# Splitting the tie marking of the last row group's attention between POOL and DVE

## What is computed

```
rel   = relu(einsum(q_idx, k_idx))           # 8 indexer heads
score = einsum(w_idx, rel)                   # one score per query and key
score = where(causal, score, -inf)
_, idx = lax.top_k(score, 256)               # 256 keys per query, the earlier key on a tie
att   = q . k[idx] / 8 - slope[head] * (t - idx)
p     = softmax(att);  out = p . v[idx]      # 8 heads, one shared key/value head
```

## Time and profile before

| | us |
|---|---|
| runs of the kernel before | 3487.24, 3488.33, 3494.06; median 3488.33 |
| profiled execution, its own time | 3487.1 |
| span of the profile | 3485.3 |
| mean granted TensorE clock | 0.974 of full speed |
| PE busy | 3214.4 (92%) |
| DVE busy | 2173.1 (62%) |
| ACT busy | 1185.6 (34%) |
| POOL busy | 715.5 (21%) |

### The profile page before, as it was taken

One profiled execution on the slowest core, in us unless ns is written; L12 is line 12 of the kernel. 1 busy time (PEld: TensorE's weight loads), 2 busy tenths in 40 slices (PEclk: granted clock), 3 DMA queues, 4 the chain that ended last, 5 costly groups with the idle time before them and its releaser, 6 DMA issues.

```text
span 3485.3 us, 41580 instructions
## 1 busy us (share of the span) xinstructions
PE 3214.4 (92%) x15045; PEld 2625.6 (75%) x15045; DVE 2173.1 (62%) x3645; ACT 1185.6 (34%) x2030; POOL 715.5 (21%) x482
## 2 busy tenths in 40 slices
PE   6991799999999999999999889999999967889998
PEld 5871688778887888768887778875888856768886
DVE  2758827688824827599894872759999988710001
ACT  3331541253335631261112753127111156521111
POOL 3430110035767000001214200000211231001212
PEclk9995899999999999999999999999999989999999
DMA  6970475569996365545555126552555510255554
GB/s 218 303 252 0 177 258 197 189 230 290 290 290 233 134 227 204 183 148 193 193 193 181 67 86 228 208 183 93 194 193 194 197 49 20 108 196 194 194 194 165
DMA packets 177565, 640.14 MB, mean 184 GB/s; under 512 B 11293, under 2 KB 95305, under 8 KB 115560
## 3 DMA queue, kind: packets, MB, share of 16 engines
q1 hardware_dynamic: 160512, 574.66, 47.8%
q10 hardware_dynamic: 16872, 63.01, 4.7%
HBM read 476.14 MB, written 161.48 MB: 183 GB/s over the span
## 4 chain that ended last, share of the span: by engine, by line
PE 65%; DVE 15%; issue 12%; ACT 5%; DMA 2%; POOL 1%; DVEq 0%; ACTq 0%; SPq 0%; POOLq 0%
PE PS L1385 14%; PE PS L1356 13%; PE PS L1358 13%; PE PS L1357 13%; DVE flags L1145 2%; DVE probs L1245 2%; PE PS L1504 2%; PE PS L1370 1%; DVE W L1130 1%; PE PS L1371 1%; PE PS L1372 1%; ACT probs L806 1%; DVE PT L1253 1%; DVE W L1253 1%; PE PS L1339 1%
## 5 line engine op out<-in xcount | busy, mean ns | idle before, releaser
L1145 DVE TENSOR_SCALAR_CACHE_REDUCE flags<-W,cand 128x1408 uint8<-128x1408 f32 (+3 forms) x462 | 683.4, 1479 | 53.7 <-DVE cand L1172 40.0
L1385 PE MATMUL PS<-WS,HT 128*128 128x512 f32 x2088 | 483.4, 392 | 5.2 <-POOL WS L452 3.0
L1385 PEld LDWEIGHTS PS<-WS,HT 128*128 128x128 f32 x2088 | 394.3, 189 | 88.3 <-issue 3.8
L523 POOL TENSOR_TENSOR TMP<-TMP 128x512 f32<-128x512 f32 x88 | 114.7, 1304 | 1539.4 <-ACT TMP L875 1539.4
L1356 PE MATMUL PS<-HF,WS 128*128 128x512 f32 x1072 | 418.1, 390 | 4.4 <-DVE HF L939 2.5
L1358 PE MATMUL PS<-HF,WS 128*128 128x512 f32 x1072 | 417.8, 390 | 0.0
L1357 PE MATMUL PS<-HF,WS 128*128 128x512 f32 x1072 | 417.8, 390 | 0.0
L452 POOL TENSOR_TENSOR WS<-RAW,WS 128x1024 fp32r<-128x1024 f32 x116 | 279.6, 2410 | 612.7 <-ACT WS L595 581.5
L1356 PE MATMUL PS<-HT,WS 128*128 128x512 f32 x824 | 325.7, 395 | 0.8 <-POOL WS L452 0.8
L1358 PE MATMUL PS<-HT,WS 128*128 128x512 f32 x824 | 321.4, 390 | 0.0
L1357 PE MATMUL PS<-HT,WS 128*128 128x512 f32 x824 | 321.1, 390 | 0.0
(11 more groups left out here) (218 smaller groups left out, 6040.7 us busy)
## 6 DMA issues: line engine op xcount, KB each, us to landing
WS<-split_weights_scratch SPq DMA_DIRECT2D x234, 1024.0 KB, 4.8
split_weights_scratch<-WS SPq DMA_DIRECT2D x116, 1024.0 KB, 5.0
W<-split_weights_scratch SPq DMA_DIRECT2D x114, 1024.0 KB, 4.8
RAW<-in_w_in SPq DMA_DIRECT2D x34, 512.0 KB, 6.0
RAW<-in_w_ffn_gate SPq DMA_DIRECT2D x22, 512.0 KB, 6.3
RAW<-in_w_ffn_up SPq DMA_DIRECT2D x22, 512.0 KB, 6.3
RAW<-in_w_ffn_down SPq DMA_DIRECT2D x22, 512.0 KB, 5.7
W<-in_x ACTq DMA_DIRECT2D x4, 2048.0 KB, 11.7
```

What stands on the lines that cost most here:

```text
L523: nc.gpsimd.tensor_tensor(out=TMP[:, s, :], in0=TMP[:, s, :], in1=TMP[:, 2 + s, :], op=ALU.mult).then_inc(h_prod, 1)
L1145: step(nc.vector.tensor_scalar(flags[:, 0:n], SC[:, t, 0:n], cand[:, t:t + 1].bitcast(f32), 0.0, op, ALU.add, accum_out=count[:, t:t + 1]))
L1385: ins = mm(PS[:, 2 * t + half, :], lhs, split(c, w_part)[:, half * 512:(half + 1) * 512], start=first and part == 0 and w_part == 0, stop= ...
```

## The change

For the last group only, POOL makes the tie flags, the rank test, the product and the kept flags of each unit, and DVE is left with the scan and the carry. DVE's part comes after both heads of a turn. POOL's tie flags of a unit are issued after the unit before it is finished, and after `finish_rows` for the first unit of tile 2. Two semaphores are added. Groups 0 to 2 are as they were.

```diff
@@ gpsimd, stage C
                         for s, w in units(b):
                             t = b % RT
-                            pool.wait_ge(marked, MASK_BASE[g] + (t - 1) * (g + 1) + s // 512 + 1)
                             sc = SC[:, t, s:s + w]
+                            if g + 1 == GROUPS:
+                                u = (t - 1) * (g + 1) + s // 512 + 1
+                                tie, rank, kth = ties[:, 0, 0:w], ties[:, 1, 0:w], cand[:, t:t + 1].bitcast(f32)
+                                pool.wait_ge(m0_ready, (g + 1) * (g + 2) // 2)
+                                nc.gpsimd.tensor_scalar(tie, sc, kth, None, ALU.is_equal).then_inc(tie_ready, 1)
+                                pool.wait_ge(tie_ready, u)
+                                pool.wait_ge(ranked, u)
+                                chained(nc.gpsimd.tensor_scalar(rank, rank, room[:, t:t + 1], None, ALU.is_le))
+                                chained(nc.gpsimd.tensor_tensor(out=tie, in0=tie, in1=rank, op=ALU.mult))
+                                chained(nc.gpsimd.tensor_scalar(sc, sc, kth, None, ALU.is_le))
+                                chained(nc.gpsimd.tensor_tensor(out=sc, in0=sc, in1=tie, op=ALU.subtract))
+                            else:
+                                pool.wait_ge(marked, MASK_BASE[g] + (t - 1) * (g + 1) + s // 512 + 1)
                             chained(nc.gpsimd.tensor_scalar(sc, sc, -BIG, float(s - b * P), ALU.mult, ALU.add))
@@ vector
+            def rank_ties(t, b, u):
+                n = (t - 1) * (b // RT + 1) + u + 1
+                w = units(b)[u][1]
+                tie, rank = ties[:, 0, 0:w], ties[:, 1, 0:w]
+                dve.wait_ge(tie_ready, n)
+                ins = nc.vector.tensor_tensor_scan(rank, tie, tie, carry[:, 0:1] if u else 0.0, ALU.add, ALU.bypass)
+                if u + 1 < len(units(b)):
+                    chained(ins)
+                    ins = nc.vector.tensor_copy(carry[:, 0:1], rank[:, w - 1:w])
+                ins.then_inc(ranked, 1)
@@ vector, stage C, turn i
-                        marking = t < RT and u_mark < U and not marks_ahead(g)
+                        marking = t < RT and u_mark < U and g == 0
@@ vector, stage C, at the end of turn i
                         while marking and step < MARKS:
                             mark(t, RT * g + t, u_mark, step)
                             step += 1
+                        if g + 1 == GROUPS and t < RT:
+                            rank_ties(t, RT * g + t, u_mark)
```

More of the change, by code:

```diff
@@ L222, in build_block @@
         bit_step, topk_done, dist_ready = sem("bit_step"), sem("topk_done"), sem("dist_ready")
+        tie_ready, ranked = sem("ties_found"), sem("ties_ranked")
         mark_step, marked0, marked, m0_ready, m_ready, s_psum, s_masked, exp_done = sem("mark_step"), sem("first_keys_marked"), sem("keys_marked"), sem("first_mask_ready"), sem("mask_ready"), sem("s_psum"), sem("scores_masked"), sem("exp_done")
```

## The result

The changed kernel took 3495.34 us (median of 20 runs) against 3488.29 us for the kernel before (20 runs): ratio 1.0016, 95% interval 1.001 to 1.0023. It is slower by 7.05 us, just over what can be told from no change. The forecast was 3498 us with a range from 3486 to 3516. The profiled execution of the changed kernel took 3495.57 us, its span is 3493.8.

What follows compares the result with a forecast made beforehand. The prediction took DVE to bound the marked turns, then PE. Gain -20.3, border waits +17.4, finish_rows wait +12.3 and PE's clock +1.5 make +10.9 us: forecast 3498 us, range 3486 to 3516.

Steps and rivals of the forecast that it cites:

- both mechanisms: In the last group, DVE waits for POOL's masks at new row tiles (17.4 us) and behind `finish_rows` (12.3 us).
- marking of the kernel before: In the last group's turns, all marking was said to cost 23.1 us, 20.3 of it gained by the change.
- scan and carry, exposed: At the end of turns, 0.25 us of the 1.4 us left on DVE stays exposed, 2.8 us in 11 turns.
- waits at the borders: At each new row tile, DVE stands still for POOL's mask: 4.8, 6.3 and 7.8 us.
- wait behind `finish_rows`: At the end of turn 4, the scan waits 12.8 us for tie flags that POOL makes after `finish_rows`.
- work that runs ahead, and PE's clock: At the four waits, 0.5 us off each for copies and transposes; one low-clock stretch adds 1.5 us in turn 4.
- the cheap rival: POOL's comparisons cost only what immediate-scalar work does, so waits are shorter: +6.0 us, 3493 us; chance 0.23.
- the prediction's upper bound of 24.5: Bound on the gain in the last group's turns: all nominal time of what leaves DVE comes off, 24.5 us.
- The ring: Rival: POOL's and DVE's cycle per unit outlasts a turn, so inner turns wait: 3505 to 3533 us; chance 0.17.
- The faster rival: Inner turns fall to DVE's own work, 10.9 us for 14 tiles: -12.7 us, 3480 with cheap comparisons; chance 0.09.
- Absorbed waits: Rival: PE and ACT run ahead of a stalled DVE, four times 1.5 us more off: 3492 us; chance 0.06.
- Contention of POOL: In the last group's turns, POOL's work beside DVE's remaining instructions was said to add nothing.

Runs made afterwards that it cites:

- e5: The changed kernel without any marking of row tiles 1 to 3 of the last group, on both engines; ratio 0.991 to the kernel before, stage 198.56 us.
- e8: The changed kernel profiled and timed again, unaltered; ratio 1.0012 to the kernel before, last group's attention stage 232.24 us.
- e9: As e6, but with the scan and carry behind the first head of a turn; ratio 0.9961 to the kernel before, stage 212.43 us.
- e7: The changed kernel with one more, unused comparison per unit on POOL; ratio 1.0042 to the kernel before, stage 244.56 us.
- e1: The changed kernel with finish_rows run behind all of POOL's masks in the last group; ratio 0.9982 to the kernel before, stage 221.04 us.
- e6: As e5, but DVE does scan and carry at each turn's end, waiting for nobody; ratio 0.9924 to the kernel before, stage 201.14 us.
- e11: As e1, but DVE marks the last unit of each row tile, POOL the other nine; ratio 0.9938 to the kernel before, stage 210.76 us.

## Why the prediction was right, and where it was off

**The direction and both mechanisms** are as forecast. The total is nearer than its terms: 8 us of error one way met 5 us the other way, and that is luck. The waits were priced from rows in which no comparison on POOL stood, and came out almost exactly:

| term | forecast, us | measured, us | from |
|---|---|---|---|
| marking of the kernel before | 23.1 | 28.5 | before less e5 |
| scan and carry, exposed | 2.8 | about 0 | inner turns: changed, e5 |
| waits at the borders | 4.8, 6.3, 7.8 | 5.01, 6.48, 7.96 | changed |
| wait behind `finish_rows` | 12.8 | 12.30 | changed |
| work that runs ahead, and PE's clock | -2.0 + 1.5 | +4.3, of it 1.1 in turn 0 (e8: +2.0) | changed less e5 less waits |
| sum | +10.9 | +7.6 | stage |

**The price of a comparison**: 1.5 us by L480, measured 1.57 for each of the three. The Trainium skill (GPSIMD Engine Reference, Engine selection) has one-input work at roughly line rate. The trace disagrees for a pointer scalar, 1.57 us against 0.62 for L516 with immediates. So the cheap rival fell at its premise.

**The term that was mis-sized is the gain.** "All the marking costs 21.6 us there, and I put 1.5 on the turns at either end": it was 25.2 and 3.3. A straight line between turns of 12 and of 16 tiles, from different groups, put the turns of 13 to 15 tiles up to 0.8 us too long, most of all at and behind a border (10.81 in e5 from reciprocal 3 to 4 and 11.03 from 4 to 5, forecast 11.5 and 11.8). The same step took the exposed part of the scan as 0.25 us a turn. It was nil, for the reason given, the 1.21 us idle behind L1245. Both errors made the change look worse than it was, 8 us together.

The 28.5 us even lie above the prediction's upper bound of 24.5, the nominal time of what leaves DVE. That bound took the scan's cost as fixed, but the change also moved the scan from mid-turn to the turn's end. e9, with the scan alone in mid-turn, is 14.6 us shorter than the kernel before and 13.9 longer than e5. By that, an estimate, about half of the gain came from the instructions that left and half from the scan's new place; no run has the scan at the turn's end with the rest still on DVE. The kernel before also had low-clock stretches of its own in these turns, 0.79 in 2828 to 2836 and in 2856 to 2864, which e5 hasn't.

**A term of the other sign hid half of it.** I took 0.5 us off each wait for work that runs ahead, and priced one stretch of low clock. Each of the four waits had one. The granted clock in the 4 us in which work was back was 0.71 (from 2844), 0.50 (from 2868), 0.50 (from 2912) and 0.50 (from 2970), and the interval from reciprocal 12 to 13, which has no marking at all, took 14.21 us against 12.74 before. The row from which the term was priced followed no long pause: PE's idle times in the 10 us ahead of 2830 were 0.3 to 1.4 us each.

**The rivals.** The ring did not bind at 1.57 us, and it did bind when e7 added one comparison; its threshold of 1.85 us was put a little too high, since the turns of 13 tiles are shorter than I had them. The faster rival, turns of DVE's bare work, didn't happen: inner turns of 14 tiles fell to 11.6 us and not to 10.9. Absorbed waits are refuted by e1. Contention of POOL with what DVE keeps in these turns showed nothing in the changed kernel: the scans of 512 keys took 1.22 to 1.28 us. The prediction's reason holds, that POOL is waiting for the scan: in e6, where POOL doesn't wait, the same scan took 3.19 and 2.15 us. e11 shows the same for the rank test.

## What to carry to other kernels

Work that moves to a slower engine must be asked two things: is its last link now directly ahead of a consumer, and what does that engine do between this piece and the next? Here the moved work itself was hidden, and the queue's older job and the three borders cost more than the engine time that was freed. And a short lump of work costs nothing or its whole length by its place in the loop (11.3 us in eleven turns by the stages of e9 and e6, about 13 without `finish_rows` beside the scans), so put it behind the last instruction that feeds the other engines' chain.

## What the runs showed of the hardware

- POOL's one-input instruction on 128x512 takes 1.57 us with a pointer scalar, whatever the operation (equal, less or equal) and the type (fp16 or fp32), and 0.62 us with two immediates. L480's multiplication, of the same form, took 2.86 us for twice the elements; the prediction had taken the comparison's price from it.
- PE stood for 3.96, 11.89, 5.21 and 7.02 us at the four waits, and in the 4 us in which work was back its granted clock was 0.71, 0.50, 0.50 and 0.50. The four low stretches, with what runs ahead of them already taken off, cost 2 to 3 us in this stage (an estimate: +2.0 in e8, +4.3 less turn 0's 1.1 in the changed kernel).
- A DVE rank test on two SBUF tiles took 1.58 us beside POOL's work in e11 and 0.75 undisturbed. A scan on SBUF tiles took 3.19 us when POOL's two-input L482 had begun 0.26 us before it (e6), and 1.28 undisturbed. The mask addition, which reads PSUM, took 1.20 to 1.23 us beside the same POOL work.
